# adaLN weights in strips of 1024 columns, and a reordered first stage, in a one-core hybrid decoder kernel

## The chip, the cores and the metric

The kernel runs on one core of a Trainium2 chip. The metric is the device time of one execution in microseconds; smaller is better. The kernel before takes 1625.23 us (median of three runs, 1624.48 to 1626.66).

## The reference, cut to what matters

One inference step of a two-layer decoder trunk for 512 prompt tokens and 8 x 8 sample tokens, 576 columns in all, with 1024 channels. Everything is float32. Both groups share all weights.

```
c     = silu([c_prompt; c_sample])                  # 9 vectors of 1024
mods  = c @ w_ada + b_ada                           # w_ada is 1024 x 16384: 16 groups of 1024
norm(x, g, shift, scale) = rmsnorm(x, g) * (1 + scale) + shift

layer 0:  h = norm(x);  a = h @ w_pw1 + b;  u = a[:1024] * sigmoid(a[1024:])
          y = causal depthwise conv of width 31 over [prev rows, u] + b
          x += gate * (silu(layernorm(y)) @ w_pw2)
          x += gate * swiglu(norm(x))               # FFN of width 2816
shared:   keys and values from one projection of norm(x)
layer 1:  x += gate * sparse_attention(norm(x));  x += gate * swiglu(norm(x))
out:      norm(x), the keys and values, the last conv rows
```

The `prev rows` of the 8 sample sequences are an input, `state_conv` (240 rows of 1024). The shift and scale of the very first norm are the first 2048 columns of `mods`; the later groups are needed one after the other, up to the final norm.

## The kernel before, in words

Channels lie on the 128 partitions, in 8 chunks; the 576 tokens are columns, split in halves of 288 for the matmuls. Each float32 product is made of three products of rounded parts: a weight tile of 128 columns ("unit") is loaded into `raw`, ScalarE makes its high part `wh` (`split_hi`), VectorE the low part `wl` (`split_lo`), and TensorE runs `dense` (line 2310) over 8 k steps. Five programs, one per engine queue, are written out in order by hand; semaphores join them, and each engine runs its own list strictly in that order. A DMA is issued from the list of SP, ScalarE or GpSimd, and a wait in such a list holds everything behind it.

**The adaLN strips.** `w_ada` is read in 32 strips of 512 columns, each in two pieces of 4 k chunks (1 MB), through a ring of three buffers (`load_ada`, line 535, on SP). TensorE multiplies a piece with `strip_half` (line 2333): 4 k x 4 column groups, each a 128x32 weight tile (the 9 vectors, padded to 32) against 128 moving columns, the four groups in four 32-column tiles of the array. ScalarE copies the finished row out of PSUM, TensorE transposes it (`turn_strip`), and ScalarE adds the bias in four copies into `mods` (`strip_out`, line 941). Five strips belong to the first stage (the fourth's last half and the fifth run inside the first dense product), thirteen run in the convolution stage, one stands in the layer norm, one at the first FFN's start, and twelve between the FFN's pairs of units. Bank 7 is shared between the turned strips and the convolution of the sample rows, which is why TensorE waits there for ScalarE's bias copies (lines 2517, 2537, 2554).

**The first stage.** GpSimd loads the x rows; TensorE transposes them (`block_in`); ScalarE squares, VectorE adds squares, TensorE sums them over partitions (`sum_chunk`), ScalarE takes the root (`root0`), VectorE the reciprocal. VectorE then makes the norm in two halves of four chunks, `norm0(0)` and `norm0(1)` (line 1724), with ScalarE making the high parts (`norm0_hi`). TensorE's first dense product (two units at once, line 2510) takes chunk after chunk as they come, and does other work ahead of its k steps (`first_strips`, line 2481): ahead of the second k step the last half of the fourth strip and its turn, ahead of the fifth `block_in(5)`, the transposes of the first 120 rows of `state_conv`.

```
for g in range(4):                          # VectorE, line 1711: ahead of split_lo(0)
    for sh in range(4):
        V.tensor_copy(wd4[...], wd_k[...]).then_inc(S("vec_dve"), 1)
...
pool.wait_ge(S("vec_dve"), 4 + 16)          # GpSimd, line 724
pool.wait_ge(lo_ready, 2)
for j in range(2):                          # two tap tiles (taps4), line 727
    nc.gpsimd.tensor_tensor(taps4[:, j % 2], ...)
pool.wait_ge(ada_used, 2 * STRIPS_FIRST - 1)
for bk in range(5, 7):
    load_rows(bk)                           # state_conv, line 702
```

The 16 copies lay the convolution's tap weights out for TensorE; the tap tiles are first used at unit 4. ScalarE's part of `norm0(0)` is `norm0_hi(0)` to `(2)`, the copy of the fourth strip's row (`strip_out(3, None)`, line 1120), `norm0_hi(3)`. VectorE's fourth `low` waits for `norm0_hi(3)`.

Of the kernel before, what the change touches and what calls it, by code (L numbers as in the profile page):

```python
# [23 lines left out]
P = 128  # L24
# [130 lines left out]
STRIP = 512  # L155
N_STRIP = 16 * D // STRIP
# [5 lines left out]

ORDER = [0, 2, 1, 3] + list(range(4, N_STRIP))
# [9 lines left out]
S_LN, S_PW2 = N_STRIP - STRIPS_FFN, N_STRIP - STRIPS_FFN + 1  # L175
STRIP_AFTER = {3 * (i // 2) + i % 2: S_PW2 + 1 + i for i in range(STRIPS_FFN - 2)}
STRIP_ROW = {s_ + 1: n for s_, n in STRIP_AFTER.items()}
STRIP_TURNED = {s_ + 2: n for s_, n in STRIP_AFTER.items()}
ADA_LATE = 2 * (N_STRIP - STRIPS_FFN)
# [13 lines left out]
def KVI(n):  # L193

    return PROMPTS[n]
# [88 lines left out]
def build(nc, a, o, c):  # L284

    ctx = ExitStack()
    with ctx:
# [79 lines left out]
        rA = region(RING_ADA * 4 * STRIP * 4)  # L367
        ada = at("ada", [P, RING_ADA, 4, STRIP], rA)
        rX = rA + RING_ADA * 4 * STRIP * 4 - half_k
        assert 2 * 4 * STRIP * 4 + rA <= rX  # L370
# [21 lines left out]
        assert o3 + 1312 <= rA + RING_ADA * 4 * STRIP * 4  # L392
# [25 lines left out]
        ada_rows = [at(f"adarow{i}", [P, 4, P], (rMu, rS)[i]) for i in range(2)]  # L418
# [58 lines left out]
        def row_of(s_):  # L477

            return ada_rows[s_ >= STRIPS_FIRST + 2][:, s_ % 4, :]
# [5 lines left out]
        def strip_bank(s_):  # L485

            return ps[:, 3 if s_ == 1 else 6, 0:P]
# [11 lines left out]
        ada_in = [S(f"ada_in{i}") for i in range(3)]  # L499
# [24 lines left out]
        def ada_at(n):  # L524

            return n % RING_ADA if n < ADA_LATE else (n - ADA_LATE) % 2

        def wait_ada(eng, n):

            if n < ADA_LATE:  # L530
                eng.wait_ge(ada_in[n % RING_ADA], 16 * (n // RING_ADA + 1))
            else:
                eng.wait_ge(ada_in[ada_at(n)], 16 * (ADA_LATE // RING_ADA + (n - ADA_LATE) // 2 + 1))

        def load_ada(sp, n):
# [4 lines left out]
            landed = ada_in[ada_at(n)]  # L540
            sp.dma_start(ada[:, ada_at(n)], wada[:, k0:k0 + 4, c0:c0 + STRIP]).then_inc(landed, 16)
# [49 lines left out]
        def _(sp):  # L591
# [36 lines left out]
            strips(2 * (S_PW2 + 1))  # L628
# [267 lines left out]
        def _(act):  # L896
# [44 lines left out]
            def strip_out(s_, turned):  # L941

                if s_ is not None:
                    act.wait_ge(ada_used, 2 * s_ + 2)
                    if s_ >= 4:
                        act.wait_ge(ada_tr, s_ - 3)
# [2104 lines left out]
```

## Time and profile before

| | |
|---|---|
| median of three timed runs | 1625.23 us (1624.48 to 1626.66) |
| span of the profiled execution, first to last instruction | 1621.3 us |
| time of the profiled execution beside its span | not given by the page; the median lies 3.9 us above the span |
| mean granted TensorE clock | 0.991 |
| TensorE busy | 1546.5 us, 95% of the span |
| VectorE, ScalarE, GpSimd busy | 67%, 48%, 12% |
| first dense matmul | 42.3 us from the span's start |

How to read it: times of rows are microseconds from the span's start, unless marked ns. PE is TensorE's matmuls, PEld its weight loads, DVE VectorE, ACT ScalarE, POOL GpSimd, SP the engine that issues most DMAs; a q behind a name is the engine's queue, which issues DMAs. An L with a number is a line of the kernel. The float32 matmuls of a strip or a convolution leave two records each. The granted clock is a share of full speed (1.00 is 2.4 GHz, 0.50 is 1.2 GHz).

### The profile page before, as it was taken

The numbers are of one execution on the slowest core, as the hardware profiler recorded it, in microseconds if no ns is written. First come the engines' busy times: TensorE is split into PE (matmuls) and PEld (weight loads), VectorE is DVE, ScalarE is ACT, GpSimd is POOL, SyncE is SP. The second block draws the span as 40 slices with busy tenths as digits, with TensorE's granted clock in tenths as the row PEclk, the third lists the DMA queues.
The fourth block names the chain that finished last, engine by engine and source line by source line (L and its number), as shares of the span: only waits on it lengthen the run. The fifth ranks groups of instructions, "written<-read, shape, count | busy, mean of one in ns | idle before, by whom it ended". The sixth has DMA issues, their size and how long they took to land.

```text
span 1621.3 us, 34765 instructions
## 1 busy us (share of the span) xinstructions
PE 1546.5 (95%) x13929; PEld 1405.1 (87%) x13929; DVE 1091.2 (67%) x2242; ACT 782.5 (48%) x1655; POOL 192.3 (12%) x330
## 2 busy tenths in 40 slices
PE   4999989999999999999999999999999999999997
PEld 3899769899999999999999655555889999999996
DVE  4889956966757657675262467666468586875866
ACT  4566765643535525443223556555355353552544
POOL 2001320000000000312000255434000000000000
PEclk8999999999999999999999999999999999999998
DMA  9899642254546646464232500110421422333321
GB/s 309 260 292 302 189 130 84 62 162 125 186 143 217 213 129 191 129 175 118 59 79 86 146 27 2 53 40 16 118 65 53 117 79 81 103 89 88 99 79 59
DMA packets 238205, 200.68 MB, mean 124 GB/s; under 512 B 8210, under 2 KB 196962, under 8 KB 237776
## 3 DMA queue, kind: packets, MB, share of 16 engines
q1 hardware_dynamic: 230768, 174.61, 36.2%
q0 software_dynamic: 6976, 23.78, 5.0%
q8 instruction: 111, 1.82, 0.5%
q14 instruction: 46, 0.38, 0.1%
q10 hardware_dynamic: 304, 0.10, 0.0%
HBM read 188.87 MB, written 11.20 MB: 123 GB/s over the span
## 4 chain that ended last, share of the span: by engine, by line
PE 79%; DVE 8%; ACT 5%; issue 4%; DMA 2%; POOL 1%; DVEq 0%; SPq 0%; ACTq 0%; POOLq 0%
PE ps L2328 32%; PE ps L2660 26%; PE ps L2308 4%; PE ps L2379 4%; PE ps L2344 2%; PE ps L2832 2%; DMA ada<-in_w_ada_dram 2%; PE ps L2785 2%; PE ps L2713 2%; PE ps L2525 1%; DVE t L1585 1%; PE ps L2904 1%; POOL Pp L870 1%; DVE wl L1517 1%; ACT Hh L987 1%
## 5 line engine op out<-in xcount | busy, mean ns | idle before, releaser
L907 ACT ACTIVATE wh<-raw 128x1024 fp32r<-128x1024 f32 (+2 forms) x129 | 118.4, 922 | 274.3 <-PE ps L2328 254.3
L2660 PE MATMUL ps<-Hh,bh 128*128 128x288 f32 x608 | 180.5, 297 | 1.0 <-DVE t L1993 1.0
L2660 PE MATMUL ps<-Hh,bl 128*128 128x288 f32 x608 | 179.0, 294 | 0.0
L2660 PE MATMUL ps<-Hl,bh 128*128 128x288 f32 x608 | 179.0, 294 | 0.0
L2328 PE MATMUL ps<-Hh,wh 128*128 128x288 f32 (+1 forms) x688 | 151.7, 302 | 3.8 <-ACT u_s L1085 2.0
L2328 PE MATMUL ps<-Hh,wl 128*128 128x288 f32 (+1 forms) x688 | 148.4, 297 | 0.0
L2328 PE MATMUL ps<-Hl,wh 128*128 128x288 f32 (+1 forms) x688 | 148.2, 297 | 0.0
L1517 DVE TENSOR_TENSOR wl<-raw,wh 128x1024 fp32r<-128x1024 f32 (+2 forms) x129 | 135.8, 1053 | 16.9 <-ACT wh L907 16.5
L2328 PE MATMUL ps<-ah,wh 128*128 128x288 f32 x656 | 141.1, 297 | 0.9 <-issue 0.9
L2328 PE MATMUL ps<-al,wh 128*128 128x288 f32 x656 | 140.5, 296 | 0.0
L2328 PE MATMUL ps<-ah,wl 128*128 128x288 f32 x656 | 140.4, 296 | 0.0
L2660 PE MATMUL ps<-Th,bh 128*128 128x288 f32 x456 | 134.8, 296 | 0.3 <-issue 0.3
L2660 PE MATMUL ps<-Tl,bh 128*128 128x288 f32 x456 | 134.5, 295 | 0.0
L2660 PE MATMUL ps<-Th,bl 128*128 128x288 f32 x456 | 134.1, 294 | 0.0
L1883 DVE TENSOR_TENSOR bl<-Sf,bh 128x512 fp32r<-128x512 f32 x152 | 103.3, 685 | 20.2 <-ACT bh L924 20.2
L2328 PEld LDWEIGHTS ps<-Hh,wh 128*128 128x128 f32 (+1 forms) x688 | 111.2, 190 | 6.2 <-issue 3.6
L2660 PEld LDWEIGHTS ps<-Hh,bh 128*128 128x128 f32 x608 | 114.4, 188 | 2.2 <-issue 1.8
L1676 DVE TENSOR_TENSOR rtmp<-ps,mods 128x64 f32<-128x64 f32 x72 | 16.2, 225 | 147.4 <-PE ps L2328 133.9
L2660 PEld LDWEIGHTS ps<-Hl,bh 128*128 128x128 f32 x608 | 114.1, 188 | 0.0
L2660 PEld LDWEIGHTS ps<-Hh,bl 128*128 128x128 f32 x608 | 114.1, 188 | 0.0
L1259 ACT ACTIVATE Z<-ps 128x288 f32<-128x288 f32 x152 | 62.0, 408 | 106.9 <-PE ps L2660 104.0
L924 ACT ACTIVATE bh<-Sf 128x512 fp32r<-128x512 f32 x152 | 94.6, 625 | 36.2 <-DVE Sf L1899 15.0
(391 smaller groups left out, 3887.5 us busy)
## 6 DMA issues: line engine op xcount, KB each, us to landing
ada<-in_w_ada_dram SPq DMA_DIRECT2D x64, 1024.0 KB, 8.4
raw<-in_ffn_w_up_dram SPq DMA_DIRECT2D x88, 512.0 KB, 4.9
raw<-in_conv_w_pw_dram SPq DMA_DIRECT2D x24, 512.0 KB, 9.5
raw<-in_ffn_w_down_dram SPq DMA_DIRECT2D x32, 384.0 KB, 3.5
raw<-in_ffn_w_down_dram SPq DMA_DIRECT2D x32, 320.0 KB, 3.2
raw<-in_w_kv_dram SPq DMA_DIRECT2D x12, 512.0 KB, 4.2
out_win_sample_dram<-in_state_win_dram POOLq DMA_DIRECT2D x8, 512.0 KB, 4.5
C<-in_cache_kv_dram POOLq DMA_DIRECT2D x32, 128.0 KB, 4.0
```

The costliest lines, as they stand in the source:

```text
L907: A(wh[:, u % RING, 0:K, 0:w], raw[:, u % RING, 0:K, 0:w], ACT.Copy).then_inc(hi_ready, 1)
L924: A(bh[:, b], src, ACT.Copy).then_inc(S("part_hi"), 1)
L1259: A(z[:, at_], ps[:, bank, 0:HT], ACT.Copy).then_inc(S("z_copy"), 1)
L1517: V.tensor_tensor(wl[:, u % RING, 0:K, 0:w], raw[:, u % RING, 0:K, 0:w], wh[:, u % RING, 0:K, 0:w].bitcast(F32), ALU.subtract).then_inc(lo ...
L1883: V.tensor_tensor(bl[:, b], src, bh[:, b].bitcast(F32), ALU.subtract).then_inc(S("part_lo"), 1)
L2308: return nc.tensor.transpose(out, in_, ident[0:in_.shape[0], 0:in_.shape[0]])
L2328: last = M(ps[0:w, 2 * s + h, 0:HT], wt[:, s, k, 0:w], rt[:, k, h * HT:(h + 1) * HT], start=(k == 0 and i == 0), stop=(k == K - 1 and i == 2))
L2344: last = M(strip_bank(s_)[32 * g:32 * g + 32], cpad[:, 4 * hf + k, :], ada[:, ada_at(n), k, g * P:g * P + P], start=(hf == 0 and k == 0), ...
L2379: last = M(ps[:, 2 * s + h, 0:HT], wt[:, s, k, :], rt[:, k, h * HT:(h + 1) * HT], start=(k == 0 and i == 0), stop=(k == K - 1 and i == 2))
L2660: last = M(ps[:, bank, 0:HT], wt[:, blk, k], rt, start=(j in (0, 1, 2, 6) and k == 0 and i == 0), stop=(k == 3 and i == 2), skip_group_che ...
L2713: last = M(ps[:, 6 + t, 0:n], w1s[t][:, j, :], cp[:, j % 8, 0:rows_, j // 8:j // 8 + NCS], start=(j == 0), stop=(j == LC // 2 - 1))
L2785: last = M(ps[:, 2 * (k % 2) + par, 0:L], qT[rows_, 2 * kv + a // 2, P * i:P * i + P], keys[rows_, 2 * br + kv // 2, 0:L], start=True, sto ...
```

## The change

- A strip is now half of a wide strip of 1024 columns. A piece is 2 k chunks x 1024 columns, still 1 MB; there are still 64 pieces. `strip_half` runs 2 k x 4 groups with 256 moving columns. A wide strip is copied out once, turned with two transposes, and its bias is added in eight copies. The first two wide strips hold the first norm's shift and scale, each piece loaded by two DMAs. The strip of the first FFN's start and one of the FFN's strips move: one half strip now stands between two units of pw2.
- The first five pieces have a buffer each (two of them in space of `u_p`, whose memset moves behind the fifth use on GpSimd).
- TensorE sums squares ahead of the half strips; ScalarE loads the root's table before `split_hi(0)`; VectorE's 16 tap copies stand between `norm0(0)` and `norm0(1)`.
- Some semaphores are shared (`a0_ln_r`, `conv_zmask`), with the counts moved on.

```diff
-STRIP = 512
-N_STRIP = 16 * D // STRIP
+STRIP = 1024
+WIDE_STRIPS = 16 * D // STRIP
+N_STRIP = 2 * WIDE_STRIPS
...
-S_LN, S_PW2 = N_STRIP - STRIPS_FFN, N_STRIP - STRIPS_FFN + 1
-STRIP_AFTER = {3 * (i // 2) + i % 2: S_PW2 + 1 + i for i in range(STRIPS_FFN - 2)}
+S_LN, S_PW2 = N_STRIP - STRIPS_FFN, N_STRIP - STRIPS_FFN + 2
+STRIP_AFTER = {3 * (i // 2) + i % 2: S_PW2 + 1 + i for i in range(STRIPS_FFN - 3)}
...
+ADA_BUF = [0, 1, 2, 3, 4] + [(n - 5) % 3 for n in range(5, ADA_LATE)] + [(n - ADA_LATE) % 2 for n in range(ADA_LATE, 2 * N_STRIP)]
...
         def load_ada(sp, n):
-            if n >= RING_ADA:
-                sp.wait_ge(ada_used, n - RING_ADA + 1 if n < ADA_LATE + 2 else n - 1)
-            c0, k0 = ORDER[n // 2] * STRIP, n % 2 * 4
...
+            before = [k for k in range(n) if ADA_BUF[k] == ADA_BUF[n]]
+            if before:
+                sp.wait_ge(ada_used, before[-1] + 1)
+            w, k0 = n // 4, n % 4 * 2
+            landed, buf = ada_in[ADA_BUF[n]], ada_buf[ADA_BUF[n]]
+            if w < 2:
+                for v in range(2):
+                    c0 = v * D + w * D // 2
+                    sp.dma_start(buf[:, :, v * D // 2:(v + 1) * D // 2],
+                                 wada[:, k0:k0 + 2, c0:c0 + D // 2]).then_inc(landed, 16)
             else:
+                sp.dma_start(buf, wada[:, k0:k0 + 2, w * STRIP:(w + 1) * STRIP]).then_inc(landed, 16)
...
             # GpSimd
-            nc.gpsimd.memset(u_p[:, :, 0:CW - 1], 0.0).then_inc(S("const"), 1)
...
             pool.wait_ge(S("vec_dve"), 4 + 16)
             pool.wait_ge(lo_ready, 2)
+            pool.wait_ge(ada_used, 5)
+            nc.gpsimd.memset(u_p[:, :, 0:CW - 1], 0.0).then_inc(S("const"), 1)
             for j in range(2):
                 nc.gpsimd.tensor_tensor(taps4[:, j % 2], ...)
...
             def strip_out(s_, turned):
-                if s_ is not None:
+                if s_ is not None and s_ % 2:
...
-                    A(row_of(s_), strip_bank(s_), ACT.Copy).then_inc(ada_row, 1)
-                if turned is not None:
-                    act.wait_ge(ada_tr, turned + 1)
-                    for k in range(4):
+                    A(row_of(s_ // 2), strip_bank, ACT.Copy).then_inc(ada_row, 1)
+                if turned is not None and turned % 2:
+                    w = turned // 2
+                    act.wait_ge(ada_tr, w + 1)
+                    for k in range(8):
...
             # ScalarE, first stage
             square0(0, 4)
-            strip_out(0, None)
             square0(4, DC)
+            act.wait_ge(S("const"), 2)
+            A(scrap[:], epst[:], ACT.Sqrt).then_inc(S("st_tb"), 1)
+            split_hi(0)
             strip_out(1, None)
-            split_hi(0)
-            act.wait_ge(S("vec_dve"), 3)
-            strip_out(None, 0)
             split_hi(1)
             root0()
+            act.wait_ge(S("vec_dve"), 3)
             strip_out(None, 1)
-            strip_out(2, None)
-            strip_out(None, 2)
...
             # VectorE
-            wd_k = wdT[:].rearrange("p (k c) -> p k c", c=DC)
-            for g in range(4):
-                for sh in range(4):
-                    V.tensor_copy(wd4[...], wd_k[...]).then_inc(S("vec_dve"), 1)
             split_lo(0)
             split_lo(1)
...
             norm0(0)
+            wd_k = wdT[:].rearrange("p (k c) -> p k c", c=DC)
+            for g in range(4):
+                for sh in range(4):
+                    V.tensor_copy(wd4[...], wd_k[...]).then_inc(S("vec_dve"), 1)
             norm0(1)
             split_lo(2)
...
             # TensorE: strip_half
-                for k in range(4):
+                for k in range(2):
+                    kk = n % 4 * 2 + k
                     for g in range(4):
-                        last = M(strip_bank(s_)[32 * g:32 * g + 32], cpad[:, 4 * hf + k, :], ada[:, ada_at(n), k, g * P:g * P + P],
-                                 start=(hf == 0 and k == 0), stop=(hf == 1 and k == 3))
+                        last = M(strip_bank[32 * g:32 * g + 32].rearrange("p (j f) -> p j f", j=2), cpad[:, kk, :],
+                                 ada_buf[ADA_BUF[n]][:, k, :].rearrange("p (j q) -> p j q", j=2)[:, :, g * P:g * P + P],
+                                 start=(kk == 0), stop=(kk == DC - 1))
...
             # TensorE: turn_strip, odd strips only
-                tr(ps[:, 7, 0:P], row_of(s_)).then_inc(ada_tr, 1)
+                for j in range(2):
+                    last = tr(ps[:, 7, j * P:j * P + P], row_of(w)[:, j * P:j * P + P])
+                last.then_inc(ada_tr, 1)
...
             # TensorE, first stage
             strip_half(1, 0)
-            strip_half(1, 1)
...
             sum_chunk(sqb[:, 0, :], 0, S("st_c0"), DC - 3, bank=4)
+            strip_half(1, 1)
+            pe.wait_ge(S("a0_ln_r"), 6)
+            sum_chunk(sqb[:, 4, :], 4, S("st_c0"), DC - 3, bank=4)
             pe.wait_ge(S("vec_dve"), 3)
-            turn_strip(0)
-            pe.wait_ge(S("st_a0"), 6)
-            sum_chunk(sqb[:, 4, :], 4, S("st_c0"), DC - 3, bank=4)
             turn_strip(1)
             strip_half(2, 0)
             strip_half(2, 1)
-            turn_strip(2)
             strip_half(3, 0)
...
+            def late_strip(m):
+                if m == RING:
+                    strip(S_LN + 1)
+                elif m == RING + 1:
+                    turn_strip(S_LN + 1)
...
-            updated(U_PW2, Hh, Hl, 0, None, RING, first_pw2)
+            updated(U_PW2, Hh, Hl, 0, None, RING, first_pw2, between=late_strip)
```

## Rows read from the trace of the kernel before

**Rows 1.** the page, part 1: busy time, share of the span, instructions

```profile
PE 1546.5 (95%) x13929; PEld 1405.1 (87%) x13929; DVE 1091.2 (67%) x2242; ACT 782.5 (48%) x1655; POOL 192.3 (12%) x330
```

**Rows 2.** timeline, TensorE, 20 to 53 us: start, us, instructions, idle before

```profile
25.95 1.93 PE L2344 MATMUL ps<-ada,cpad 128*32 128x128 f32 x32 [3.18 <-DMA ada<-in_w_ada_dram]
...
30.10 1.85 PE L2366 MATMUL ps<-sqb,ones 128*128 128x288 f32 x4
...
39.76 1.93 PE L2344 MATMUL ps<-ada,cpad 128*32 128x128 f32 x32 [2.33 <-DMA ada<-in_w_ada_dram]
...
42.31 0.82 PE L2328 MATMUL ps<-Hh,wh 128*128 128x288 f32 x2 [0.62 <-DVE Hl L1751]
...
45.36 1.08 PE L2344 MATMUL ps<-ada,cpad 128*32 128x128 f32 x32
...
51.80 0.98 PE L2308 MATMUL ps<-ident,srows 120*128 120x120 f32 x8
```

**Rows 3.** timeline, VectorE, 20 to 53 us

```profile
26.90 3.50 DVE L1713 COPY wd<-wdT 32x64 f32<-32x64 f32 x16
...
34.28 3.75 DVE L1718 RECIPROCAL r<-r 128x576 f32<-128x576 f32 x1 [0.92 <-ACT r L958]
...
47.43 0.75 DVE L1751 SCALAR_TENSOR_TENSOR Hl<-t,mods,Hh 128x512 fp32r<-128x512 f32 x1 [2.37 <-ACT Hh L1114]
```

**Rows 4.** timeline, ScalarE, 0 to 75 us

```profile
33.52 0.72 ACT L958 ACTIVATE r<-ps,epst 128x576 f32<-128x576 f32 x1
...
47.30 0.74 ACT L952 ACTIVATE mods<-ps,badaT 128x9 f32<-128x9 f32 x4
```

**Rows 5.** timeline, GpSimd, 0 to 75 us

```profile
33.53 3.88 POOL L727 TENSOR_TENSOR taps<-sel,wd 128x1024 f32<-128x1024 f32 x2 [25.77 <-DVE wl L1517]
...
42.02 1.10 POOL L702 DMA_DIRECT2D srows<-in_state_conv_dram  x2 [4.61 <-PE ps L2344]
```

**Rows 6.** the tile of the state rows, its two loads

```profile
DMA to landing us min/median/max: 8.8/10.0/11.2
```

**Rows 7.** the page, part 6: DMA issues, KB each, median us to landing

```profile
raw<-in_ffn_w_down_dram SPq DMA_DIRECT2D x32, 384.0 KB, 3.5
...
out_win_sample_dram<-in_state_win_dram POOLq DMA_DIRECT2D x8, 512.0 KB, 4.5
```

**Rows 8.** timeline, SP's queue, 56 to 62 us

```profile
57.04 0.37 SPq L541 DMA_DIRECT2D ada<-in_w_ada_dram  x1
```

**Rows 9.** stretches: us, busy per engine, granted clock, DMA share, GB/s

```profile
28.00:40.00 12.00, 6.72 (x83) 4.57 (x87) 9.92 (x19) 6.76 (x20) 3.88 (x2) 0.78 1.00 339
...
62.30:64.30 2.00, 0.05 (x1) 0.00 (x0) 2.00 (x5) 1.92 (x3) 0.00 (x0) 1.00 0.97 272
...
65.60:69.10 3.50, 3.50 (x17) 3.50 (x16) 3.50 (x6) 0.00 (x0) 0.00 (x0) 0.51 0.86 284
69.10:72.30 3.20, 3.20 (x26) 3.11 (x24) 3.20 (x6) 0.00 (x0) 0.00 (x0) 1.00 0.09 27
```

**Rows 10.** timeline, TensorE, later stretches: strips, turns, convolutions

```profile
89.44 1.10 PE L2506 MATMUL ps<-us,taps 128*32 128x64 f32 x64
90.36 1.93 PE L2344 MATMUL ps<-ada,cpad 128*32 128x128 f32 x64
92.22 0.33 PE L2308 MATMUL ps<-ident,adarow 128*128 128x128 f32 x1
...
165.73 0.30 PE L2308 MATMUL ps<-ident,adarow 128*128 128x128 f32 x1 [1.59 <-ACT adarow L947]
...
208.56 7.07 PE L2525 MATMUL ps<-up,taps 128*32 128x512 f32 x64 [1.45 <-ACT mods L952]
...
215.43 1.10 PE L2506 MATMUL ps<-us,taps 128*32 128x64 f32 x64
```

**Rows 11.** timeline, VectorE, 203 us: the last tap tile

```profile
203.57 1.22 DVE L1787 TENSOR_TENSOR taps<-sel,wd 128x1024 f32<-128x1024 f32 x1
```

**Rows 12.** the page, part 5: one group of ScalarE, idle time and its releaser

```profile
L1259 ACT ACTIVATE Z<-ps 128x288 f32<-128x288 f32 x152 | 62.0, 408 | 106.9 <-PE ps L2660 104.0
```

More of the change, by code:

```diff
@@ L161 @@
 ROW_BANK = [0, 1, 2, 0, 1, 2, 2]
-ORDER = [0, 2, 1, 3] + list(range(4, N_STRIP))
 STRIPS_AHEAD = 1
@@ L416, in build @@
         rS = region(DC * TS * 4)
-        ada_rows = [at(f"adarow{i}", [P, 4, P], (rMu, rS)[i]) for i in range(2)]
+        ada_rows = [at(f"adarow{i}", [P, 2, STRIP // 4], (rMu, rS)[i]) for i in range(2)]
         fs = at("fs", [P, DC, TS], rS)
@@ L498, in build @@
         tile_done, tile_free = S("tile_done"), S("tile_free")
-        ada_in = [S(f"ada_in{i}") for i in range(3)]
+        ada_in = [S(f"ada_in{i}") for i in range(5)]
+        ada_buf = [ada[:, 0], ada[:, 1], ada[:, 2], ada_extra[:, 0], ada_extra[:, 1]]
         pair_in = [S(f"pair_in{i}") for i in range(2)]
@@ L627, in _ @@
             assert u_next == U_PW2 + RING
-            strips(2 * (S_PW2 + 1))
+            strips(2 * S_PW2)
             def plain(to):
@@ L658, in _ @@
                     plain(U_WO + RING)
+                else:
+                    plain(U_PW2 + RING + 3)
+                    strips(2 * (S_PW2 + 1))
                 plain(u_down(layer, 0))
@@ L733, in add_chunk @@
             def add_chunk(j):
-                pool.wait_ge(S("conv"), (CW + 1) * (j + 1))
+                pool.wait_ge(S("conv_zmask"), (CW + 1) * (j + 1))
                 pool.wait_ge(S("cs_ev"), j + 1)
@@ L1767, in _ @@
             dve.wait_ge(S("const"), 4)
-            taps = S("conv")
+            taps = S("conv_zmask")
             odd_sum = r[:, 0:TP]
@@ L1857, in _ @@
                 dve.wait_ge(S("ln_rms"), h + 1)
-                V.reciprocal(half(r, h), half(r, h)).then_inc(S("ln_r"), 1)
-                dve.wait_ge(S("ln_r"), h + 1)
+                V.reciprocal(half(r, h), half(r, h)).then_inc(S("a0_ln_r"), 1)
+                dve.wait_ge(S("a0_ln_r"), 6 + h + 1)
                 dve.wait_ge(S("ln_yc"), 2 * DC)
@@ L2178, in weights @@
                 if i == 0:
-                    V.tensor_tensor(z, z, maskc[:].unsqueeze(1).to_broadcast([P, G, NCP]), ALU.mult).then_inc(S("zmask"), 1)
-                    dve.wait_ge(S("zmask"), sum(KVI(k)[1] == 0 for k in range(n + 1)))
+                    V.tensor_tensor(z, z, maskc[:].unsqueeze(1).to_broadcast([P, G, NCP]), ALU.mult).then_inc(S("conv_zmask"), 1)
+                    dve.wait_ge(S("conv_zmask"), (CW + 1) * (DC - 3) + sum(KVI(k)[1] == 0 for k in range(n + 1)))
                 dve.wait_ge(W, 4 * n + 3)
@@ L2588, in first_pw2, with updated @@
                 last.then_inc(tile_done, 1)
-                turn_strip(S_LN)
-            def updated(u0, hi, lo, g, ready, tiles, begin=None, after=None):
+            def updated(u0, hi, lo, g, ready, tiles, begin=None, after=None, between=None):
                 if after:
@@ L2600, in updated @@
                     if m >= tiles:
+                        if between:
+                            between(m)
                         if after and m < RING:
```

99 lines of the change are left out of this document (47 added, 52 removed).

## Prediction

> **What bounds the kernel now.** I read the page first: TensorE is busy for 1546.5 of 1621.3 us [rows 1]. So almost everywhere TensorE's own instruction stream is the time, and a saved matmul counts in full. The exception is the first stage, before the first dense product (line 2510), where the timelines of the engines have to be read against each other. There are two chains there. By one, TensorE waits for the seventh piece of the adaLN weights until 39.76 and works it off until 41.69; by the other, VectorE's reciprocal, which starts at 34.28, and the norm behind it let the first dense matmul start at 42.31, 0.62 us after that [rows 2, 3]. They end nearly together, so shortening one alone buys 0.6 us. The second thing to see is a chain that costs nothing today: GpSimd makes two tap tiles from 33.53 on (3.88 us), issues the two state-row loads at 42.02, and the first lands 8.8 us later, at 50.8 [rows 5, 6]. TensorE transposes these rows inside the first dense product, ahead of its fifth k step, at 51.80, with no idle time before it [rows 2]. That is one microsecond of slack.
>
> All sums are made against the profiled execution. It has a span of 1621.3 us; the page gives no other time of its own, and the median of the three timed runs, 1625.23, lies 3.9 us above that span. I take this 3.9 as unchanged.
>
> **Part by part.** D is the start of the first dense matmul, 42.31 before.
>
> 1. Five piece buffers. The order of the pieces on SP's queue is unchanged and so are the bytes ahead of the seventh piece. From 28 to 40 us the DMA engines are already full (share 1.00) [rows 9], so an earlier issue only lengthens the queue. I leave the landing at 39.76. Each of the first eight pieces is now two loads: eight more issues at 0.37 us each [rows 8], 3.0 us of SP's time, behind a queue that is full.
>
> 2. Sums ahead of the strips, root table early. The second sum starts at 30.10; moved behind the half strip that ends at 27.88 (25.95 + 1.93), it ends 2.2 us earlier [rows 2], and the table load no longer stands before the root, which runs at 33.52 [rows 4]. The root could come at about 30.0, the reciprocal 3.5 us earlier, and VectorE's chain would allow D = 38.8. The weights do not: 39.76 + 1.93 = 41.69. So D moves by -0.6. Bounds: 0, and -3.5 if the weights come earlier after all.
>
> 3. Tap copies between the norm's halves. This is the edit that decides. The 16 copies (3.50 us, at 26.90) move from before the splits to behind `norm0(0)` [rows 3]. The last instruction of `norm0(0)` is the fourth `low`, at 47.43, and it has waited 2.37 us for ScalarE, whose part stands behind the copy of a strip row that needs the half strip at 45.36, inside the dense product [rows 2, 3]. It ends at D + 5.8 (48.1 - 42.3), hence the copies at D + 9.3. GpSimd's queue waits for all 16 copies (line 724), and behind that wait stand a small memset, moved there (not priced), the two tap tiles (3.88) and only then the loads of the state rows [rows 5]. They are issued at D + 9.3 + 3.9 = D + 13.2, while TensorE wants the rows landed at D + 9.5 (51.80 - 42.31). Before, they were issued at D - 0.3. Landing: 8.8 us there, under full queues; from 3.5 us (384 KB on SP's queue) and 4.5 us (512 KB on GpSimd's) up where the queues are shorter [rows 6, 7]. I take 5.0, near the short ones: SP's next weight load, at 57.04 before the change, waits for the strip half behind these rows, so SP has nothing new to send while TensorE stands [rows 8]. Stall: 13.2 + 5.0 - 9.5 = +8.7; bounds 7.2 (landing in 3.5) and 12.5 (in 8.8). Behind `block_in(5)` there is no other wait: `norm0(1)` starts at D + 9.3; the first half took from 38.0, the reciprocal's end, to 48.2, with the wait of 2.4 in it [rows 3], so 7.8 without; the second ends near D + 17, before the rows land at D + 18.2.
>
> 4. The clock after the stall. From 65.6 to 69.1, just after a wait of 2 us with TensorE idle (62.3 to 64.3), the granted clock is 0.51 (1.2 GHz): 17 matmuls in 3.5 us, against 26 in 3.2 us at 1.00 [rows 9]. At full clock the 17 would take 2.1 us, so such a stretch costs 1.4. I add one: +1.4, bounds 0 and 2.8.
>
> 5. Strips of 1024 columns. A strip of 512 columns is 64 matmul records of 128 columns in 1.86 us start to start (90.36 to 92.22), 29.1 ns each [rows 10]. The same columns become 32 records of 256. No row shows that form with 128 input rows. The nearest are the convolutions with the same 32-column tiles: 64 records of 64 columns in 0.92 us (14.4 ns each), 64 of 512 columns in 6.87 us (107.3 ns) [rows 10]. By them 256 columns cost 57.5 or 53.7 ns, and a strip 1.84 or 1.72 us. I take 0.10 us saved per strip, between them, times the 28 strips outside the first stage: -2.8; bounds -0.5 and -3.9. Turns: half as many, each with two transposes; I price this at zero. The late strip between pw2 products replaces one in the FFN: zero, the count is the same.
>
> The Trainium skill (TensorE: Matmul & The Clock Gate, section "The mechanism" of Part 3) says that weight loads overlap with matmuls in flight only when their row groups differ. These four tiles share all rows, so by that rule every record would show its weight load, and halving the records would save much more than 2.8 us. The trace disagrees: 64-column records take 14.4 ns each [rows 10], half of the 128-column ones, so columns alone set the time, and the rule is not followed here.
>
> 6. Two waits go. Half of the turns vanish, among them the one at 165.73 that waited 1.59 us for ScalarE's row copy; and ScalarE has no four bias copies left in front of the last convolution, which waited 1.45 us for them at 208.56 [rows 10]. Together -3.0. What is late next is VectorE's last tap tile, ready at 204.8 (203.57 + 1.22): the convolution at 208.56 can move by 3.8 at most relative to VectorE [rows 11]. The 13 strips before it bring 1.3 more, so 0.5 of the 4.3 is lost. Bounds: 0 and -3.0.
>
> 7. ScalarE now does eight bias copies in one go, 0.75 us more than four [rows 4], in some FFN pairs, with the next z copy behind them. ScalarE waited 104.0 us on TensorE ahead of its 152 z copies, 0.68 us each [rows 12], so this hides: 0; without cover six times 0.75, +4.5.
>
> **Sum.** -0.6 + 8.7 + 1.4 - 2.8 - 3.0 + 0.5 = +4.2: span 1625.5, median 1629.4.
>
> **Rivals.**
> A. The stall is there, but the other terms come out at their good ends: D -3.5 because the pieces land earlier, strips -3.9, waits -2.5, stall 7.2, clock 1.4. That is -1.3: 1623.9. For it: VectorE's chain really frees 3.5 us. Against it: a full queue up to the seventh piece.
> B. Faster: the state rows do not hold TensorE, since the copies finish early in `norm0`'s idle time (VectorE stands 2.37 us before the fourth `low` [rows 3]) and the rows land while TensorE still waits for the second half of the norm. Then only the gains count: -0.6 - 2.8 - 2.5 = -5.9, 1619.3. It decides once stall and clock together cost under 2.7 us, that is once the loads are issued before about D + 6 instead of D + 13. Against it: the copies stand behind the fourth `low` in VectorE's order, and VectorE runs its queue in order.
> C. The loads meet queues as full as before (8.8 us) and the bursts of point 7 do not hide: stall 12.5 and +4.5. Then -0.6 + 12.5 + 1.4 - 2.8 - 2.5 + 4.5 = +12.5: 1637.7; the full queue alone, without the bursts, gives 1633.2.
> D. The change does not do what it says: the wide strips stream no faster (-0.5) and the two waits come back under another name (0). Then -0.6 + 8.7 + 1.4 - 0.5 = +9.0: 1634.2.
>
> **Chances.** Forecast 0.52, A 0.20, B 0.10, C 0.10, D 0.08. Within 0.2% (3.25 us, about what a measurement of this kernel can tell from no change) are A and about a quarter of the forecast's own spread (1626.5 to 1632.5), 0.33 in all; slower are the rest of it, C and D, 0.57; faster is B, 0.10. The range goes from 1622.5, a little below A, to 1636.5, above D, and leaves out B and the end of C.
>
> **What would show it.** Right: in the changed kernel's GpSimd timeline the loads from the conv state stand some 13 us behind the first dense matmul; TensorE's timeline has an idle time of 7 to 13 us before the transposes of `srows`, put down to that DMA, and the granted clock falls to 0.5 behind it; later strips take 1.72 to 1.84 us for the same columns; the idle times at the turn and at the last convolution are gone. D lies near 41.7. Wrong: no idle time before `srows` (then B), D near 39 (then A, or more), a landing of 9 us (C), new waits on ScalarE in the FFN (point 7), or strips below 1.7 us.

## The result, and the profile after

The changed kernel takes 1633.62 us (median of 12 runs, 1630.46 to 1640.58), the kernel before 1625.88 on the same chip: +7.7 us, ratio 1.0050, 95% interval 1.0040 to 1.0061. Slower, as forecast, and inside the range; the forecast was +4.2. The profiled spans differ by 9.0 us, 1630.3 against 1621.3. The page, part 1, of the changed kernel, beside [rows 1]: 1024 fewer matmul records, and TensorE still busy 5 us longer.

```profile
PE 1551.6 (95%) x12905; PEld 1384.2 (85%) x12905; DVE 1095.3 (67%) x2242; ACT 780.4 (48%) x1639; POOL 192.8 (12%) x330
```

TensorE's timeline of the changed kernel, first stage, answering to [rows 2]:

```profile
36.42 1.94 PE L2347 MATMUL ps<-ada,cpad 128*32 128x256 f32 x16 [0.78 <-DMA ada<-in_w_ada_dram]
38.29 0.85 PE L2333 MATMUL ps<-Hh,wh 128*128 128x288 f32 x2
...
56.31 1.06 PE L2313 MATMUL ps<-ident,srows 120*128 120x120 f32 x4 [8.60 <-DMA srows<-in_state_conv_dram]
```

The first dense matmul starts 4.0 us earlier than before (38.29 against 42.31), and then TensorE stands for 8.6 us before the transposes of the state rows, where it did not stand at all. What made it wait is in the timelines of VectorE ([rows 3]) and GpSimd ([rows 5]) and in the view of the tile ([rows 6]), all of the changed kernel:

```profile
29.78 3.75 DVE L1718 RECIPROCAL r<-r 128x576 f32<-128x576 f32 x1
...
43.08 0.75 DVE L1751 SCALAR_TENSOR_TENSOR Hl<-t,mods,Hh 128x512 fp32r<-128x512 f32 x1 [2.52 <-ACT Hh L1121]
43.75 3.50 DVE L1767 COPY wd<-wdT 32x64 f32<-32x64 f32 x16
...
47.52 0.42 DVE L1736 TENSOR_TENSOR fs<-x,acoef 128x256 f32<-128x256 f32 x1
47.97 2.07 DVE L1739 TENSOR_TENSOR fs<-fs,r 128x256 f32<-128x256 f32 x1
50.08 2.07 DVE L1741 TENSOR_TENSOR fs<-fs,mods 128x256 f32<-128x256 f32 x1
...
53.73 0.74 DVE L1751 SCALAR_TENSOR_TENSOR Hl<-t,mods,Hh 128x512 fp32r<-128x512 f32 x1
```
```profile
47.80 4.07 POOL L736 TENSOR_TENSOR taps<-sel,wd 128x1024 f32<-128x1024 f32 x2
51.81 1.11 POOL L710 DMA_DIRECT2D srows<-in_state_conv_dram  x2
```
```profile
DMA to landing us min/median/max: 4.5/5.2/5.9
```

Read it as a chain: the copies end at 47.25, GpSimd makes its tiles until about 51.8 and only then issues the loads, the first lands 4.5 us later. That is the forecast chain with its numbers: issue at D + 13.5 (forecast 13.2), landing 4.5 (5.0), stall 8.6 (8.7).

Behind the stall the clock falls. Windows of the changed kernel, columns as in [rows 9], over the stretch behind the stall and over the later one behind a 2 us wait, which the kernel before has too:

```profile
56.00:62.00 6.00, 5.69 (x30) 5.70 (x31) 3.26 (x4) 3.98 (x5) 0.00 (x0) 0.61 0.16 40
...
70.90:74.40 3.50, 3.50 (x15) 3.50 (x16) 3.29 (x5) 0.79 (x1) 0.00 (x0) 0.51 0.89 307
```

From the state rows to the next half strip TensorE needs 6.14 us (56.31 to 62.45), where it needed 4.10 before (51.80 to 55.90): 2.0 us for the slow clock there (granted 0.50 from 56.3 to 60.7 us, 1.00 from there to 62.4).

**Where the 9.0 us lie.** The same TensorE instruction is looked up in both timelines and the times subtracted; each step is the change of that difference.

| up to | before | after | difference | step |
|---|---|---|---|---|
| first dense matmul | 42.31 | 38.29 | -4.0 | -4.0 |
| transposes of the state rows | 51.80 | 56.31 | +4.5 | +8.5 |
| end of the slow clock, third dense product | 68.72 | 75.44 | +6.7 | +2.2 |
| last prompt convolution | 208.56 | 211.77 | +3.2 | -3.5 |
| sums of the first end stage, behind the FFN | 710.92 | 716.26 | +5.3 | +2.1 |
| first product of the attention | 911.42 | 916.85 | +5.4 | +0.1 |
| output projection | 1146.12 | 1154.70 | +8.6 | +3.2 |
| end | 1621.3 | 1630.3 | +9.0 | +0.4 |

The fourth step is the two waits of [rows 10], which are gone. TensorE's timeline of the changed kernel, at the strip that stood ahead of the turn at 165.73 and at the last convolution, has no idle time:

```profile
168.78 1.91 PE L2347 MATMUL ps<-ada,cpad 128*32 128x256 f32 x32
170.62 0.53 PE L2333 MATMUL ps<-Hh,wh 128*128 128x288 f32 x2
...
211.77 0.64 PE L2532 MATMUL ps<-up,taps 128*32 128x512 f32 x4
```

The fifth step was not forecast. Its rows (end stage: TensorE, ScalarE, and the issues of GpSimd and SP), changed kernel:

```profile
716.26 0.75 PE L2381 MATMUL ps<-mu,ones 128*128 128x288 f32 x2 [2.08 <-DVE mu L1549]
```
```profile
711.56 1.06 ACT L916 ACTIVATE wh<-raw 128x1024 fp32r<-128x1024 f32 x1 [6.61 <-DMA raw<-in_w_kv_dram]
```
```profile
694.60 1.19 POOL L843 DMA_DIRECT2D w1k<-in_w_cmp_dram  x1 [15.61 <-DMA raw<-in_ffn_w_down_dram]
```
```profile
695.52 0.37 SPq L520 DMA_DIRECT2D raw<-in_w_kv_dram  x1
```

and the same issues before:

```profile
694.24 1.19 POOL L834 DMA_DIRECT2D w1k<-in_w_cmp_dram  x1 [7.75 <-DMA raw<-in_ffn_w_down_dram]
```
```profile
692.41 0.37 SPq L516 DMA_DIRECT2D raw<-in_w_kv_dram  x1
```

Before, SP's first unit of `w_kv` was issued 1.8 us ahead of GpSimd's two loads of `w_cmp` (2 MB) and landed 3.9 us after its issue; now it is issued 0.9 us behind the first of them, lands 16.0 us after its issue, and ScalarE, VectorE and TensorE wait for it in turn. GpSimd is early because the last FFN unit, on whose landing `w_cmp` waits, lands 3.3 us after its issue instead of 6.0. The order of issue goes with the landing in all 14 profiles here: `w_kv` lands after 15.3 to 16.5 us in the nine that issue it behind `w_cmp`, after 3.7 to 4.3 in the five that issue it ahead. Why the FFN unit lands sooner is argued and not tested: GpSimd's constants and cache pages follow the last strip's bias copies, are issued from 661.7 instead of 669.2, and so may be out of its way.

The seventh step is no effect of the change that these traces show. The stretches of the attention in windows (columns as in [rows 9]), before and after:

```profile
911.42:1146.12 234.70, 218.02 (x2186) 128.79 (x2187) 160.42 (x605) 137.58 (x431) 99.10 (x145) 1.00 0.18 50
```
```profile
916.85:1154.70 237.85, 221.16 (x2187) 130.93 (x2187) 160.61 (x605) 137.65 (x431) 99.21 (x145) 0.99 0.17 49
```

The number of operations is the same but for one record, TensorE is busy 3.1 us longer, and the granted clock is lower. Over the profiles of all kernels here this stretch takes 234.7 (two of them), 237.8 to 240.8, or 243.75 us (two), with edits that do not touch it. So below, single profiles are compared up to the start of the attention, and the medians and ratios give the whole.

### The profile page after: what moved, and what is told of

It reads as the page before. It is cut to its first block, busy times and chain, and to the rows that moved or that the text cites. A ratio compares the mean times of both kernels' runs of the same rounds, so it can differ in the third digit from the quotient of the medians.

```text
span 1630.3 us, 32664 instructions
## 1 busy us (share of the span) xinstructions
PE 1551.6 (95%) x12905; PEld 1384.2 (85%) x12905; DVE 1095.3 (67%) x2242; ACT 780.4 (48%) x1639; POOL 192.8 (12%) x330
## 4 chain that ended last, share of the span: by engine, by line
PE 82%; DVE 7%; ACT 4%; DMA 3%; issue 3%; POOL 1%; SPq 0%; DVEq 0%; ACTq 0%; POOLq 0%
PE ps L2333 34%; PE ps L2675 26%; PE ps L2313 5%; PE ps L2388 3%; PE ps L2347 3%; PE ps L2845 2%; PE ps L2798 2%; DMA ada<-in_w_ada_dram 2%; PE ps L2726 2%; PE ps L2532 1%; DMA raw<-in_w_kv_dram 1%; DVE t L1590 1%; PE ps L2917 1%; POOL Pp L879 1%; ACT Hh L996 1%
## 5 line engine op out<-in xcount | busy, mean ns | idle before, releaser
L2333 PEld LDWEIGHTS ps<-Hh,wl 128*128 128x128 f32 (+1 forms) x688 | 111.3, 189 | 0.2
```

The costliest lines, as they stand in the source:

```text
L2333: last = M(ps[0:w, 2 * s + h, 0:HT], wt[:, s, k, 0:w], rt[:, k, h * HT:(h + 1) * HT], start=(k == 0 and i == 0), stop=(k == K - 1 and i == 2))
```

## The experiments

Each run is one of the two kernels with the edit shown. The two columns behind its name are read from its one profile, in us from the span's start; the median is of 5 to 12 timed runs, and the ratio compares them with the kernel before, timed beside them on the same chip.

| kernel | first dense matmul | attention starts | median | ratio to before, 95% interval |
|---|---|---|---|---|
| before | 42.31 | 911.4 | 1624.86 to 1626.56 | 1 |
| changed | 38.29 | 916.9 | 1633.62 | 1.0050 (1.0040 to 1.0061) |
| e1 copies back | 42.02 | 910.1 | 1625.95 | 1.0013 (1.0002 to 1.0024) |
| e2 rows first | 38.88 | 915.1 | 1629.10 | 1.0021 (1.0012 to 1.0031) |
| e3 rows first, copies last | 38.47 | 905.8 | 1622.48 | 0.9992 (0.9981 to 1.0003) |
| e4 `w_kv` first | 38.94 | 913.5 | 1631.33 | 1.0035 (1.0022 to 1.0048) |
| e5 the copies' move alone | 42.37 | 921.8 | 1637.23 | 1.0075 (1.0062 to 1.0088) |
| e6 three buffers | 38.48 | 920.3 | 1632.75 | 1.0051 (1.0034 to 1.0068) |
| e7 narrow records | 38.27 | 920.6 | 1637.67 | 1.0072 (1.0049 to 1.0095) |
| e8 e3 and e4 together | 38.62 | 903.7 | 1619.84 | 0.9971 (0.9958 to 0.9985) |
| e9 narrow, other order | 39.69 | 919.9 | 1634.20 | 1.0049 (1.0033 to 1.0065) |
| e10 two loads a piece alone | 40.49 | 910.8 | 1624.75 | 0.9988 (0.9979 to 0.9997) |
| e11 sums and table back | 40.47 | 918.1 | 1638.61 | 1.0070 (1.0054 to 1.0086) |
| e12 e1, tap tiles late | 39.43 | 907.6 | 1624.64 | 0.9987 (0.9975 to 0.9998) |

### The stall: e5, e1, e2, e3

e5: the kernel before with one part alone.

```diff
-            <16 tap copies>          # ahead of split_lo(0)
             norm0(0)
+            <16 tap copies>
             norm0(1)
```

> The kernel before with one part of the change alone: the 16 tap copies moved between the halves of the first norm. Theory (this part makes the stall): TensorE waits 7 to 9 us before the transposes of the state rows, and its clock is at half for some 4 us behind them; the first dense matmul moves to 41.7 (the 3.5 us of copies leave VectorE's way, the seventh piece ends at 41.7). +8.6 + 2.2 - 0.6 = +10 us against the kernel before. Rival (the stall needs the rest of the change too: fuller queues, an earlier first matmul): 2 to 5 us only, +3 to +6.

TensorE's timeline of e5 at the state rows:

```profile
60.13 1.86 PE L2308 MATMUL ps<-ident,srows 120*128 120x120 f32 x8 [8.65 <-DMA srows<-in_state_conv_dram]
```

8.65 us of stall and +10.4 up to the attention: this part alone makes the stall, and more than the changed kernel's whole loss there (+5.4). The first dense matmul did not move to 41.7 as expected (42.37): VectorE's reciprocal waits for ScalarE's root in both kernels and starts at 34.28 and 34.34, so in the old order the copies cost nothing where they stood.

e1: the reverse, the copies put back in the changed kernel (the same five lines moved up).

> The changed kernel with only the 16 tap copies put back ahead of the two splits. Theory (the copies late in VectorE's queue hold GpSimd, and GpSimd the state rows): the wait of 8.6 us before the transposes of the state rows is gone, and the slow clock behind it (2.2 us) with it; the first dense matmul moves from 38.3 to about 39.0, since the reciprocal starts 1.3 us later and had 0.6 to spare. -10.1 us against the changed kernel: about 2.4 us below the kernel before. Rival (the queues, fuller now with five pieces in flight, hold the rows): they are issued near 38 and land only after 48 to 50, and 1 to 3 us of the wait stay, so about as long as the kernel before.

The state rows in TensorE's timeline of e1:

```profile
52.66 0.98 PE L2313 MATMUL ps<-ident,srows 120*128 120x120 f32 x8
```

The stall is gone, and so is the clock loss, but the first dense matmul falls back to 42.02, not to 39.0, and the total is not 2.4 us below the kernel before but 0.1% above it. VectorE, of e1:

```profile
31.51 3.74 DVE L1723 RECIPROCAL r<-r 128x576 f32<-128x576 f32 x1
35.49 0.99 DVE L1732 SCALAR_TENSOR_TENSOR acoef<-mods,vT 128x36 f32<-128x36 f32 x1 [0.24 <-DVE r L1723]
36.52 2.11 DVE L1741 TENSOR_TENSOR fs<-x,acoef 128x256 f32<-128x256 f32 x1
```

0.99 and 2.11 where the changed kernel has 0.20 and 0.43, just while GpSimd makes the tap tiles (34.47 to 38.35). e12 tests that.

e2: GpSimd's row loads ahead of its wait for the copies.

```diff
+            pool.wait_ge(lo_ready, 2)
+            pool.wait_ge(ada_used, 2 * STRIPS_FIRST - 1)
+            for bk in range(5, 7):
+                load_rows(bk)
             pool.wait_ge(S("vec_dve"), 4 + 16)
-            pool.wait_ge(lo_ready, 2)
-            pool.wait_ge(ada_used, 5)
...
-            pool.wait_ge(ada_used, 2 * STRIPS_FIRST - 1)
-            for bk in range(5, 7):
-                load_rows(bk)
```

> The changed kernel with only the two loads of the state rows moved in GpSimd's queue ahead of its wait for the copies. Theory (the rows alone hold TensorE): wait and slow clock go, -10.8 us, 3 us below the kernel before. Rival, and what I hold likelier now (the copies on VectorE hold TensorE twice: the fifth low part, for the second half of the norm, ended at 54.47, only 1.8 us before the rows): TensorE waits for that low part instead, 6.7 us, and gets its clock loss too; -2 us against the changed kernel, 5 to 6 us above the kernel before.

TensorE's timeline of e2, from the state rows on:

```profile
48.57 1.04 PE L2312 MATMUL ps<-ident,srows 120*128 120x120 f32 x8
55.26 0.85 PE L2332 MATMUL ps<-Hh,wh 128*128 128x288 f32 x2 [5.65 <-DVE Hl L1750]
```

The rows are in time, and the wait comes back at TensorE's next operation, 5.65 us for VectorE's fifth low part. The rival's mechanism holds, its total less well (-4.5 us against the changed kernel by the medians, where it had -2): the copies stood in front of two things that TensorE needs, and the rows were only the later one.

e3: e2, and the copies moved on, behind `norm0(1)`.

> As the kernel with the row loads first, and the 16 copies moved on, behind the whole norm and ahead of the third split. Theory (with neither the rows nor the norm behind the copies nothing waits): no idle time of over 0.5 us on TensorE between 38.3 and the end of the first unit, no slow clock there; -10.8 us against the changed kernel, 3 us below the kernel before. Rival (the copies only pass the wait on): the third split and the tap tiles, 3.5 us later now, hold the third dense product or the first convolution, and 2 to 4 us come back there.

The same place of e3:

```profile
48.61 0.98 PE L2312 MATMUL ps<-ident,srows 120*128 120x120 f32 x8
49.39 0.54 PE L2332 MATMUL ps<-Hh,wh 128*128 128x288 f32 x2
```

No idle time, attention 11.1 us earlier than in the changed kernel. The theory holds; the tap tiles, ready only at 62.5, hold nobody. That e3 is faster than the kernel before is not shown: its median is 2.9 us lower, but the interval of the ratio includes 1.

### Where the first dense matmul's 4 us came from: e6, e11, e10

e6: `ADA_BUF = [n % 3 for n in range(ADA_LATE)] + ...`, three buffers all through.

> The changed kernel with three piece buffers all through instead of five in the first stage. Theory B (the five buffers brought the weights in earlier, by filling the times in which three left the DMA engines short of work): the seventh piece lands near 39.5, the first dense matmul starts near 41.5 instead of 38.3, all behind it is as late: +3 us against the changed kernel. Rival O (the weights came earlier for another reason, an earlier start or the two loads a piece): 38 to 39, no change.

TensorE's timeline of e6 at the first dense matmul:

```profile
36.29 1.94 PE L2347 MATMUL ps<-ada,cpad 128*32 128x256 f32 x16 [0.69 <-DMA ada<-in_w_ada_dram]
38.48 0.82 PE L2333 MATMUL ps<-Hh,wh 128*128 128x288 f32 x2 [0.25 <-DVE Hl L1751]
```

The seventh piece lands as early as with five, 3.5 us before [rows 2]'s 39.76. Theory B falls: the five buffers bring the first dense matmul nothing. (Behind it this profile loses 3.5 us up to the attention; the median shows no loss.)

e11: the changed kernel with the order put back.

```diff
-            sum_chunk(sqb[:, 0, :], ...)
-            strip_half(1, 1)
-            sum_chunk(sqb[:, 4, :], ...)
-            turn_strip(1)
+            strip_half(1, 1)
+            sum_chunk(sqb[:, 0, :], ...)
+            turn_strip(1)
+            sum_chunk(sqb[:, 4, :], ...)
...
-            A(scrap[:], epst[:], ACT.Sqrt)     # ahead of split_hi(0)
+            A(scrap[:], epst[:], ACT.Sqrt)     # at root0
```

> The changed kernel with the two sums of squares put back behind the half strip and the turn, and the root's table load back ahead of the root. Theory (this order freed VectorE's chain): the reciprocal starts 2 to 3.5 us later than 29.8, at 32 to 33.3, the norm behind it holds TensorE, first dense matmul at 40.5 to 41.8 instead of 38.3; the copies, the rows and the stall move with it: +2 to +3.5 us against the changed kernel. Rival (the pieces set the start, as they end at 38.3 anyway): no change.

The same place of e11, and its reciprocal:

```profile
37.34 1.93 PE L2347 MATMUL ps<-ada,cpad 128*32 128x256 f32 x16 [0.76 <-DMA ada<-in_w_ada_dram]
40.47 0.82 PE L2333 MATMUL ps<-Hh,wh 128*128 128x288 f32 x2 [1.20 <-DVE Hl L1751]
```
```profile
32.43 3.75 DVE L1718 RECIPROCAL r<-r 128x576 f32<-128x576 f32 x1 [0.92 <-ACT r L969]
```

The reciprocal starts at 32.43 instead of 29.78, and the norm holds TensorE until 40.47: 2.2 of the 4.0 us are this order's, given that the copies have moved. Up to the attention 1.2 us of them are left.

e10: the kernel before, each of the first eight pieces loaded by two DMAs (the count that TensorE waits for is changed to match, not shown).

```diff
-            sp.dma_start(ada[:, ada_at(n)], wada[:, k0:k0 + 4, ...])
+            for v in range(2):       # n < 8
+                sp.dma_start(ada[:, ada_at(n), 2 * v:2 * v + 2], wada[:, k0 + 2 * v:k0 + 2 * v + 2, ...])
```

> The kernel before, in which each of the first eight pieces is loaded by two loads of 512 KB instead of one of 1 MB; nothing else is changed. Theory L (the rows of c land 2 us earlier behind smaller loads, and with them starts TensorE's whole first stage): TensorE's first operation at 7.7 to 8.3 instead of 10.1, the seventh piece ends 1 to 2 us earlier, but VectorE's chain (0.6 behind the pieces) moves too: first dense matmul 40.5 to 41.5, -1 to -2 us in all. Rival (the earlier start comes from elsewhere in the change): first operation at 10.1, no change.

TensorE's timeline of e10, its first operation and the first dense matmul:

```profile
7.75 0.35 PE L2310 MATMUL ps<-ident,rows 72*128 72x72 f32 x1 [7.75 <-ACT rows L1073]
...
35.77 1.08 PE L2346 MATMUL ps<-ada,cpad 128*32 128x128 f32 x32 [0.83 <-DMA ada<-in_w_ada_dram]
...
40.49 0.82 PE L2330 MATMUL ps<-Hh,wh 128*128 128x288 f32 x2 [3.64 <-DVE Hl L1753]
```

The first operation, the transpose of the rows of c, comes at 7.75 instead of 10.14. It lies between 7.6 and 8.3 in every kernel here with two loads a piece, and at 10.0 and 10.1 in the two with one. The seventh piece comes 4.0 us earlier, and the first dense matmul 1.8: now the norm holds it. Theory L holds; with e11, 1.8 and 2.2 us make up the 4.0. Three limits belong to that sum. Up to the state rows only 0.6 of e10's 1.8 us are left (51.18 against 51.80), as TensorE's granted clock is 0.51 from 40.4 to 46.6, where it was 0.52 from 42.3 to 45.3 before. One profile is not firm to a tenth: in the seven kernels that share the changed kernel's loads, buffers, order and VectorE work up to there, the first dense matmul starts between 38.27 and 39.69. And the parts are not independent: with the copies ahead of the splits again (e1, 42.02), the two loads and the new order together start it later than the two loads alone (e10, 40.49); e12 shows why.

### The strips: e7, e9

e7: two records of 128 columns in place of one of 256, one behind the other on the same column group.

```diff
                     for g in range(4):
-                        last = M(strip_bank[32 * g:32 * g + 32]..., <256 columns>)
+                        for j in range(2):
+                            last = M(strip_bank[32 * g:32 * g + 32, j * P:j * P + P], ..., <128 columns>)
```

> The changed kernel, in which each strip matmul of 256 columns is two of 128 columns into the two halves of the same bank; loads, turns and order as in the changed kernel. Theory C (columns alone set the time): 29.1 ns a record, 1.86 to 1.87 us for 512 columns over 8 k steps, 0 us against the changed kernel. Rival W (each record has a cost of its own, as the prediction had it): 0.1 us a strip in 28 strips, +2.8; if every record showed its weight load, far more.

e9: the same with `for j` outside `for g`.

> As the kernel with two records of 128 columns in place of one of 256 (1.95 us a strip, against 1.86 for the wide records and 1.88 for the narrow ones before the change), but each record goes to another 32-column group than the one before it: the four groups for one half, then the four for the other. Theory G (two records in a row on the same group cost 0.09 us a strip): 1.88 us a strip again, 0.6 us in 28 strips above the changed kernel. Rival N (the narrow record costs that in this layout, whatever its neighbour): 1.95 a strip, +2.5.

TensorE's timeline at one strip and the matmul behind it, in this order: the kernel before, the changed one, e7, e9; the form of [rows 10].

```profile
80.90 1.96 PE L2344 MATMUL ps<-ada,cpad 128*32 128x128 f32 x64
82.79 0.33 PE L2308 MATMUL ps<-ident,adarow 128*128 128x128 f32 x1
```
```profile
78.98 1.93 PE L2347 MATMUL ps<-ada,cpad 128*32 128x256 f32 x32
80.85 0.53 PE L2333 MATMUL ps<-Hh,wh 128*128 128x288 f32 x2
```
```profile
79.06 2.02 PE L2348 MATMUL ps<-ada,cpad 128*32 128x128 f32 x64
81.02 0.53 PE L2333 MATMUL ps<-Hh,wh 128*128 128x288 f32 x2
```
```profile
81.24 1.96 PE L2348 MATMUL ps<-ada,cpad 128*32 128x128 f32 x64
83.13 0.53 PE L2333 MATMUL ps<-Hh,wh 128*128 128x288 f32 x2
```

Start to start these are 1.89, 1.87, 1.96 and 1.89 us; the medians over the later strips of each profile 1.88, 1.86, 1.95 and 1.88. Half as many records save 0.02 us a strip, 0.6 us in 28. The other 0.07 of e7 come from two records in a row on the same group of 32 columns: e9 has the same records in another order and is back at 1.88. In e7 my theory C fell and W's number was nearly met (0.09 in 28 strips is 2.5 us), though for another reason; e9 shows the reason, theory G. These sizes are read from the strips; the ratios' intervals of e7 and e9 overlap the changed kernel's.

### The late `w_kv`, and the two mends together: e4, e8

e4: GpSimd's loads of `w_cmp`, and what it issues behind them, wait for the first unit of `w_kv`.

```diff
-            pool.wait_ge(raw_in[(U_KV - 1) % RING], 16 * ((U_KV - 1) // RING + 1))
+            pool.wait_ge(raw_in[U_KV % RING], 16 * (U_KV // RING + 1))
```

> The changed kernel, in which GpSimd's two loads of w_cmp (2 MB) wait for the landing of the first unit of w_kv, not of the unit before it. Theory (these 2 MB, issued 0.9 us ahead of w_kv where they stood 1.8 us behind it before the change, make it land late): the wait of 2.1 us at the sums of the first end stage (710 us) is gone, -2.1 us against the changed kernel, 5.5 above the kernel before. Rival (w_kv's own queue is slow, or ScalarE is): the wait stays at 1 to 2 us, no change. A cost of the edit: w_cmp lands some 10 us later; nothing of it is needed before the products of the key-value part are done.

ScalarE's timeline of e4 at the first unit of `w_kv`, and TensorE's at the sums:

```profile
706.94 1.06 ACT L916 ACTIVATE wh<-raw 128x1024 fp32r<-128x1024 f32 x1 [3.00 <-PE ps L2333]
```
```profile
713.02 0.65 PE L2381 MATMUL ps<-mu,ones 128*128 128x288 f32 x2
```

`w_kv` no longer holds ScalarE, TensorE goes into the sums without idle time, and the attention starts 3.3 us earlier than in the changed kernel, 1.0 of which this profile had already gained at the last prompt convolution, ahead of the edit; the medians differ by 2.3, though the two intervals overlap. The edit holds back the four cache pages behind `w_cmp` too, so which of these loads delayed `w_kv` is not separated.

e8: the edits of e3 and e4 together.

> The row loads first, the copies behind the whole norm, and w_cmp behind the first unit of w_kv, together. Theory (the two losses are apart, so the gains add): -10.7 - 1.8 to 2.1 against the changed kernel by the medians measured for each alone: 4.5 to 5 us below the kernel before. Rival (w_cmp comes too late now that all stands 10 us earlier, or the end stage then waits for something else): no better than the kernel with the rows first and the copies last, 3 below.

e8 is the fastest kernel here: 5.0 us below the kernel before, the interval clear of 1, and its attention starts 2.1 us ahead of e3's, the size of the wait taken away. The gains add, as the theory had it.

### VectorE beside GpSimd: e12

e1 with GpSimd's tap tiles behind the third split, the rows ahead of them.

```diff
             pool.wait_ge(lo_ready, 2)
+            <wait for ada_used, load_rows(5), load_rows(6)>
             pool.wait_ge(S("vec_dve"), 4 + 16)
-            pool.wait_ge(ada_used, 5)
+            pool.wait_ge(lo_ready, 3)
```

> The kernel with the copies back ahead of the splits (first dense matmul at 42.0, with two of VectorE's operations of the first norm at 0.99 and 2.11 us instead of 0.20 and 0.42, while GpSimd made the tap tiles), with GpSimd's tap tiles now behind the third split and the state rows ahead of them. Theory (VectorE's operations on two tensors are held while GpSimd's run): both are back at 0.20 and 0.42, first dense matmul at 39.5, -2.5 us against the kernel with the copies back. Rival (they were slow for another reason, the weights landing): no change, 42.0.

VectorE's timeline of e12, the two operations behind the reciprocal:

```profile
35.38 0.20 DVE L1732 SCALAR_TENSOR_TENSOR acoef<-mods,vT 128x36 f32<-128x36 f32 x1 [0.24 <-DVE r L1723]
35.62 0.42 DVE L1741 TENSOR_TENSOR fs<-x,acoef 128x256 f32<-128x256 f32 x1
```

0.20 and 0.42 again, the first dense matmul at 39.43, 2.6 us earlier. The theory holds. So in e1 the copies ahead of the splits cost the start mainly through the tap tiles, which then run beside the norm. The reciprocal, 1.6 us later than in the changed kernel (31.41 against 29.78), can explain what is left, 1.1 us, but that is within the spread of the first dense matmul named above.

## Why the prediction came out as it did

- **Steps 3 and 4, the stall and the clock: right.** 8.5 and 2.2 us against 8.7 and 1.4. "Behind `block_in(5)` there is no other wait" was right by little: in the changed kernel the fifth low part is ready at 54.47, only 1.8 us before the rows, and e2 shows TensorE waiting for it. It was as near as that because GpSimd's tiles held two of VectorE's operations for 1.6 us each, which the step did not count. For the same reason the second half of the norm ended at 58.25, D + 20 and not near D + 17, behind the rows; that cost nothing, because TensorE takes it chunk by chunk. The wait of 2 us that step 4 took its price from does not always slow the clock: e1 and e3 have the same wait of 2.0 us ahead of the third dense product and run on at 1.00 (65.2 to 68.5 and 61.2 to 64.5 us).
- **Step 2 failed: "The weights do not: 39.76 + 1.93 = 41.69".** I took the seventh piece's landing as fixed because the DMA engines showed a share of 1.00 over 28 to 40 us [rows 9]. A full average does not fix when the load that matters lands: with two loads a piece the rows of c, and all of the first stage behind them, came some 2 us earlier, and the piece 3 to 4 us earlier (e10). I had priced these loads as 3.0 us of SP's time and nothing else. Measured -4.0 for -0.6; the bound of -3.5 was too near too. The other half of the step was over-sized: the order freed VectorE's chain by 2.7 us (reciprocal at 32.43 in e11, 29.78 in the changed kernel) and not by 3.5. Step 1, the five buffers at nothing, held (e6).
- **Step 5 was mis-sized:** 0.02 us a strip and not 0.10, -0.6 instead of -2.8, at the low bound (-0.5). I interpolated between records of 64 and 512 columns, 57.5 and 53.7 ns for 256; measured are 58.2 ns (1.86 us for 32), above both ends and twice the 29.1 of 128 columns. The weight loads were rightly not charged: halving the records saved 0.02.
- **Step 6: right.** Both waits are gone; the stretch from 75 to 212 us gained 3.5 us, 3.0 of it forecast, and 0.3 of the rest the thirteen strips there. The 0.5 I gave back to VectorE's last tap tile was not needed. The late strip's zero held, and so did step 7's: no new wait in the FFN.
- **Not seen at all:** the late `w_kv`, +2.1. I asked what the earlier strips do to TensorE and not what GpSimd, which waits for the last of them, then issues earlier.

So the forecast sum of +4.2 became, up to the attention, +5.4: 3.4 us better at the start, 2.2 worse in the strips, 0.8 worse in the clock, 2.1 for `w_kv`, and the rest small. That the two totals lie so near is in part luck: 5.1 us of misses one way were met by 3.4 the other way. Two of the signs of being right failed: D lies at 38.3, which was named as a sign of A, and the strips take 1.86 us, where 1.72 to 1.84 were named. The nearest rival's story, D's "the wide strips stream no faster", was true, but not its "waits come back". The medians say +7.7 and the ratio +6.5 to +9.9: some 2 us above the +5.4 to +5.8 of the traces without the attention's own spread. What they are stays open; the granted clock of the attention may be lower more often in the changed kernel. The mean granted clock of whole executions fits that, with a median of 0.984 in its 12 timed runs against 0.988 to 0.989 in 66 of the kernel before, but the slow clock behind the stall is part of it, and one profile for each kernel cannot separate the two.

## What to carry to other kernels

Before moving work on one engine, list what waits behind it on every queue that it feeds, and take away the waits one after the other in thought: behind the state rows stood the norm, 1.8 us earlier, so the row loads first gave back 1.7 us up to the attention (e2), and the copies taken out of the way of both gave back 11.1 (e3). An edit can cost in one place through what it lets run side by side in another (e1, e12). Work that frees early on one engine sends off what waits for it elsewhere, so look at the DMAs that come sooner and at what they overtake (e4). A DMA share of 1.00 says that bytes flow, not that the bytes that are needed flow first (e10).

## What the runs showed of the hardware

- **VectorE held by GpSimd.** VectorE's operations on two tensors took 2.07 and 2.11 us instead of 0.42 beside GpSimd's tap tiles, about 2 us each, and were back at 0.42 when the tiles moved away (e12). The reciprocal, on one tensor, took 3.75 us in the kernel before, beside the tiles from 34.28 on, and 3.75 in the changed kernel without them. The Trainium skill (SBUF — State Buffer, section "SBUF: two separate sides") says that the two engines share a pair of ports, that an instruction of either holds it to its end, and that on VectorE's side instructions with two SBUF inputs or in a 2-port mode are concerned; these rows agree. One tensor does not make an operation safe: in e3 one with a single tensor and two columns of scalars, issued beside the tiles (56.94 to 62.53), took 2.19 us, against 0.54 in e12; no row shows the mode it ran in.

```profile
60.63 2.19 DVE L1812 TENSOR_SCALAR y<-u_p,wdT,vT 128x512 f32<-128x512 f32 x1
```

- **Order of the column groups.** A 128-column record on the same group of 32 columns as the one before it costs more: 1.95 us against 1.88 for 64 of them (e7, e9), while width alone, 128 or 256 columns, made 0.02.
- **Smaller loads at the start.** Two loads of 512 KB in place of one of 1 MB on SP's queue let the small loads of c on ScalarE's queue land some 2 us earlier: ScalarE's first operation on them starts at 7.29 in e10 and at 9.68 before. How the queues bring that about stays open.
- **The clock in the attention.** The same work took 234.7 us at a granted clock of 1.00 and 243.75 at 0.96. The stretch of e12:

```profile
907.59:1151.34 243.75, 227.08 (x2186) 134.28 (x2187) 160.94 (x605) 138.17 (x431) 99.20 (x145) 0.96 0.17 48
```

A single profile's span of this kernel can therefore differ from another by 9 us without any edit in that stretch, more than most of the effects above.
